# A Mamba-2 and gated-DeltaNet trunk step on one core: one table for Ln and Exp, the query scale folded into the outputs' scale, and the first scan chunk loaded in the projection

## What is computed

```python
q = l2norm(q) * (GDN_DK ** -0.5);  k = l2norm(k)          # rsqrt(sum of squares + EPS)
# for each chunk of tokens and each head, with state S:
o = (q * exp(gcum)) @ S + (q @ k.T * decay) @ v_new
S = S * exp(last) + (k * exp(last - gcum)).T @ v_new
# afterwards
y_gdn = rmsnorm(o, gdn_norm_w) * silu(gate)               # rsqrt(mean of squares + EPS)
```

## Time and profile before

| | us |
|---|---|
| three runs | 3535.12, 3541.09, 3542.61 |
| median | 3541.09 |
| profiled execution | 3537.88 |
| its span, first to last instruction | 3536.1 |
| mixnorm and gates | 0 to 98 |
| projection | 101 to 1151 |
| scan | 1153 to 1973 |
| running sequences | 1977 to 2206 |
| merge, output projection | 2209 to 2635 |
| ffnnorm, up, down, lastnorm | 2636 to 3536 |

### The profile page before, as it was taken

How to read it: one execution, slowest core, us unless ns; L and a number is a source line. 1 busy time by engine, 2 the same in 40 slices (tenths; PEclk the granted TensorE clock), 3 DMA queues, 4 the chain that set the end, 5 groups by cost and what they waited for, 6 DMA issues and landing times. The chain is left out here.

```text
span 3536.1 us, 53776 instructions
## 1 busy us (share of the span) xinstructions
PE 3148.2 (89%) x20442; PEld 2962.7 (84%) x20442; DVE 1559.5 (44%) x2031; ACT 993.9 (28%) x1607; POOL 447.4 (13%) x525
## 2 busy tenths in 40 slices
PE   3799999999999698989999488899886999997996
PEld 2799999999999577777778227899876999997996
DVE  5455555401010467777676443455324322333444
ACT  3232323211211244434334201333213211122333
POOL 1000000000000233333333122000000000000000
PEclk7899999999999799999999666899998999998998
DMA  1222222222222422223320522754401112215432
GB/s 70 78 97 85 97 85 97 97 85 97 85 97 75 101 59 60 59 60 85 86 66 16 165 95 77 256 202 154 150 12 63 59 68 72 72 60 198 168 128 94
DMA packets 223765, 338.78 MB, mean 96 GB/s; under 512 B 146296, under 2 KB 159336, under 8 KB 223248
## 3 DMA queue, kind: packets, MB, share of 16 engines
q1 hardware_dynamic: 217344, 311.73, 27.2%
q0 software_dynamic: 6288, 25.25, 2.0%
HBM read 243.72 MB, written 93.22 MB: 95 GB/s over the span
## 5 line engine op out<-in xcount | busy, mean ns | idle before, releaser
L521 PE MATMUL pps<-h_hi,pwh 128*128 128x358 f32 (+1 forms) x2112 | 687.9, 326 | 13.8 <-DVE pwl L586 13.8
L521 PE MATMUL pps<-h_lo,pwh 128*128 128x358 f32 (+1 forms) x2112 | 689.5, 326 | 0.0
L521 PE MATMUL pps<-h_hi,pwl 128*128 128x358 f32 (+1 forms) x2112 | 686.9, 325 | 0.0
L521 PEld LDWEIGHTS pps<-h_hi,pwh 128*128 128x128 f32 x2112 | 397.0, 188 | 13.9 <-issue 13.9
L521 PEld LDWEIGHTS pps<-h_hi,pwl 128*128 128x128 f32 x2112 | 398.5, 189 | 0.0
L521 PEld LDWEIGHTS pps<-h_lo,pwh 128*128 128x128 f32 x2112 | 397.4, 188 | 0.0
L1585 PE MATMUL u_ps<-f_hi,up_wh 128*128 128x358 f32 (+1 forms) x1056 | 344.6, 326 | 21.3 <-DVE up_wl L1577 21.3
L1585 PE MATMUL u_ps<-f_lo,up_wh 128*128 128x358 f32 (+1 forms) x1056 | 345.2, 327 | 0.0
L1585 PE MATMUL u_ps<-f_hi,up_wl 128*128 128x358 f32 (+1 forms) x1056 | 344.0, 326 | 0.0
L586 DVE TENSOR_TENSOR pwl<-pw,pwh 128x1024 fp32r<-128x1024 f32 x88 | 107.8, 1225 | 506.2 <-ACT pwh L534 500.1
L1585 PEld LDWEIGHTS u_ps<-f_hi,up_wh 128*128 128x128 f32 x1056 | 199.0, 188 | 22.3 <-issue 22.3
(11 more groups left out here) (398 smaller groups left out, 5378.7 us busy)
## 6 DMA issues: line engine op xcount, KB each, us to landing
projected<-pO SPq DMA_DIRECT2D x88, 536.0 KB, 2.8
pw<-in_w_in SPq DMA_DIRECT2D x88, 512.0 KB, 3.4
scan_chunk<-projected SPq DMA_DIRECT2D x10, 3744.0 KB, 16.8
merge_w<-in_w_out SPq DMA_DIRECT2D x72, 512.0 KB, 3.3
down_w<-in_w_down SPq DMA_DIRECT2D x48, 704.0 KB, 4.1
up_w<-in_w_up SPq DMA_DIRECT2D x44, 512.0 KB, 4.4
mixed<-scan_chunk SPq DMA_DIRECT2D x10, 1248.0 KB, 6.5
ffn<-uf SPq DMA_DIRECT2D x22, 536.0 KB, 3.0
```

The lines of the kernel that those rows point to most:

```text
L521: ins = pe.matmul(ps[:, 3 * u + n, 0:cn], l[u][:, k, :], r[:, k, c0:c0 + cn], start=(k == 0 and a == 0), stop=(k == KD - 1 and a == 2))
```

## The change

Four things are done. (1) Each norm, the gates and both scan phases begin on ACT with a load of the table `natural_log_exp_and_others`, which has Ln and Exp (and Copy, Square, Abs). In the scans it stands in place of an Ln of one element, L1111. (2) `o` isn't scaled by the query's scale any more. ACT squares the unscaled `o` as soon as it is complete. DVE squares `rs` of q at the chunk's end (one operation of 104x8), multiplies the mean square by it in `mean_square` (one more operation of 104x8), and forms the product of `rs`, 128 ** -0.5 and `ors` in `normalise` (one more), by which `o` is scaled. `be` grows from two to five rows. (3) SP loads chunk 0 and its three rows of `sel` in the projection, ahead of the "sigmoid" stage, after it has waited for the stores of both buffers; it waits for the load's end at the end of the phase. The buffer lies at the right end of SBUF. (4) The scan counts that load as done and issues only that of chunk 1.

```diff
@@ -178,6 +178,7 @@
             prime(act, squared, ln_done, rstd_done, hi_done)
+            act.preload_act_table_set("natural_log_exp_and_others")
@@ -427,7 +429,7 @@
-def project_phase(nc, d, hi, lo, scratch):
+def project_phase(nc, d, hi, lo, scratch, sums, first, sel):
@@ -454,6 +456,7 @@
         plain = pair("plain", 3)
+        first_in = Loads(nc, "p_first_in", 1, 2)
         zero = Event(nc, "p_zero")
@@ -495,7 +498,17 @@
-            stages(sp, body)
+            def load_first(kind):
+                if kind == "sigmoid":
+                    for u in range(2):
+                        sp.wait_ge(stored.sems[u], stored.at(NSCAN // 2 - 1))
+                    sp.dma_start(sel[3 * H:3 * H + 3, :, :], sums[:, 0:C].rearrange("(a h) n -> a h n", a=3)).then_inc(
+                        first_in.sems[0], 16)
+                    sp.dma_start(first[:, :, :], scratch[0:NSCAN, :, 0:C].rearrange("m p n -> p m n")).then_inc(
+                        first_in.sems[0], 16)
+
+            stages(sp, body, load_first)
+            sp.wait_ge(first_in.sems[0], first_in.at(0))
             for u in range(2):
@@ -623,7 +636,7 @@
-def scan_phase(nc, d, tab, con, scratch, mixed, sums, running):
+def scan_phase(nc, d, tab, con, scratch, mixed, sums, running, chunk0=None):
@@ -649,14 +662,14 @@
         sel = [con["selT"]] + ([] if running else [buf("sel", [P, H, C], BF16)])
-        cd = [buf(f"chunk{u}", [P, NSCAN, c]) for u in range(1 if running else 2)]
+        cd = [buf("chunk0", [P, NSCAN, c])] if running else [chunk0, buf("chunk1", [P, NSCAN, c])]
         kraw, sqr, vb, kn, kbn, kw = (buf(n, [P, HG, P]) for n in ("kraw", "sqr", "vb", "kn", "kbn", "kw"))
...
         mat = buf("mat", [P, 2, HG, c])
-        ss, rs, lg, be = buf("ss", [P, 3, HG]), buf("rs", [P, 2, 2, HG]), buf("lg", [P, 3, HG]), buf("os", [P, 2, HG])
+        ss, rs, lg, be = buf("ss", [P, 3, HG]), buf("rs", [P, 2, 2, HG]), buf("lg", [P, 3, HG]), buf("os", [P, 5, HG])
         ors = buf("ors", [P, HG])
@@ -738,7 +751,7 @@
             E("v_h1", 4 * nseq), E("v_yz", 4), E("v_yms"), E("v_ys", 4))
-        v_rq = E("v_rq")
+        v_rq, v_oqs = E("v_rq"), E("v_oqs")
         v_cm, v_km, v_qm = E("v_cm"), E("v_km"), E("v_qm")
@@ -813,8 +826,9 @@
-                for u in range(2):
-                    load(u, u)
+                sp.sem_inc(loaded.sems[0], 16)
+                sp.sem_inc(sums_in.sems[0], 16)
+                load(1, 1)
                 with sp.Fori(0, NC // 2 - 1) as i:
@@ -1108,8 +1122,7 @@
                   a_ors, a_k, a_kT, a_kbT, a_T, a_X, a_vn)
-            act.activation(lg[:, 0, 0:1], con["ones"][:, 0:1], ACT.Ln)
-
+            act.preload_act_table_set("natural_log_exp_and_others")
             act.wait_ge(zeroed.sem, zeroed.at(0))
@@ -1229,7 +1242,7 @@
                     act.activation(yg, yg, ACT.Copy, scale=yss[0:c, 3, g:g + 1]).then_inc(a_yn.sem, 1)
-                act.wait_ge(v_oq.sem, v_oq.at(r))
+                act.wait_ge(v_o2.sem, v_o2.at(r))
                 act.wait_ge(m_VN.sem, m_VN.at(r))
@@ -1244,7 +1257,7 @@
                   v_kss, v_kn, v_kbn, v_AT, v_qk, v_TT, v_km, v_T, v_TTn, v_yms, v_res, v_o1, v_S0, v_o2,
-                  v_S1, v_rq, v_oq, v_oss, v_oms, v_on, v_ys, v_yg)
+                  v_S1, v_rq, v_oqs, v_oq, v_oss, v_oms, v_on, v_ys, v_yg)
             dve.memset(ss[:, :, :], 1.0)
@@ -1279,12 +1292,19 @@
                 dve.wait_ge(v_oss.sem, v_oss.at(r))
-                dve.tensor_scalar(ss[0:c, 2, :], be[0:c, 1, :], 1.0 / P, EPS, ALU.mult, ALU.add).then_inc(v_oms.sem, 1)
-
-            def normalise(r):
+                dve.wait_ge(v_rq.sem, v_rq.at(r))
+                dve.scalar_tensor_tensor(out=be[0:c, 3, :], in0=be[0:c, 1, :], scalar=1.0 / P ** 2, in1=be[0:c, 2, :],
+                                         op0=ALU.mult, op1=ALU.mult).then_inc(v_oqs.sem, 1)
+                dve.wait_ge(v_oqs.sem, v_oqs.at(r))
+                dve.tensor_scalar(ss[0:c, 2, :], be[0:c, 3, :], EPS, None, ALU.add).then_inc(v_oms.sem, 1)
+
+            def normalise(r, u):
+                dve.wait_ge(a_ors.sem, a_ors.at(r))
+                dve.scalar_tensor_tensor(out=be[0:c, 4, :], in0=rs[0:c, u, 1, :], scalar=float(P) ** -0.5, in1=ors[0:c, :],
+                                         op0=ALU.mult, op1=ALU.mult).then_inc(v_oq.sem, 1)
                 dve.wait_ge(v_oq.sem, v_oq.at(r))
-                dve.wait_ge(a_ors.sem, a_ors.at(r))
-                dve.tensor_tensor(on[0:c, :, :], o[0:c, :, :], bcast(ors[0:c, :], P), ALU.mult).then_inc(v_on.sem, 1)
+                dve.wait_ge(v_o2.sem, v_o2.at(r))
+                dve.tensor_tensor(on[0:c, :, :], o[0:c, :, :], bcast(be[0:c, 4, :], P), ALU.mult).then_inc(v_on.sem, 1)
@@ -1386,7 +1406,7 @@
                 if not first:
-                    normalise(r - 1)
+                    normalise(r - 1, 1 - u)
                 for hb in range(2):
@@ -1469,10 +1489,7 @@
-                dve.tensor_scalar(rs[0:c, u, 1, :], rs[0:c, u, 1, :], float(P) ** -0.5, None, ALU.mult).then_inc(v_rq.sem, 1)
-                dve.wait_ge(v_rq.sem, v_rq.at(r))
-                dve.wait_ge(v_o2.sem, v_o2.at(r))
-                dve.tensor_tensor(o[0:c, :, :], o[0:c, :, :], bcast(rs[0:c, u, 1, :], P), ALU.mult).then_inc(v_oq.sem, 1)
+                dve.tensor_tensor(be[0:c, 2, :], rs[0:c, u, 1, :], rs[0:c, u, 1, :], ALU.mult).then_inc(v_rq.sem, 1)
@@ -1482,7 +1499,7 @@
             mean_square(last_round)
-            normalise(last_round)
+            normalise(last_round, last_place)
             gate_out(last_round, last_place)
@@ -2040,6 +2057,7 @@
                    "naccT": sb("t_naccT", [P, T], BF16)}
+            scanned = to_scan.enter_context(ExitStack())
             with ExitStack() as to_project:
@@ -2052,8 +2070,10 @@
                         "p (b q) -> p b q", b=NB)))
-                project_phase(nc, d, hi, lo, scratch)
-            scan_phase(nc, d, tab, con, scratch, mixed, sums, False)
+                chunk0 = scanned.enter_context(nc.sbuf_tensor("chunk0", [P, NSCAN, C], F32, side="right"))
+                project_phase(nc, d, hi, lo, scratch, sums, chunk0, con["selT"])
+            scan_phase(nc, d, tab, con, scratch, mixed, sums, False, chunk0)
+            scanned.close()
             scan_phase(nc, d, tab, con, scratch, mixed, sums, True)
```

## The result

| | before | changed |
|---|---|---|
| median, us | 3541.38 (3535.12 to 3542.61, 4 runs) | 3518.11 (3516.34 to 3522.13, 4 runs) |
| ratio, 95% interval | | 0.9939 (0.9922 to 0.9957) |
| profiled execution, us | 3537.88, span 3536.1 | 3517.55, span 3515.4 |

The changed kernel is 23 us faster (20.7 by the spans of the two profiled executions). The forecast was 3510 with a range of 3499 to 3522: right in sign and range, 8 us too good by the median, 10 by the sum (30.8 forecast, 20.7 between the two profiled executions).

A forecast was written before the change was run, and what follows sets the result against it. PE (busy 89%) was taken to bound the kernel, the scan being a latency chain partly paced by DVE. Gains of 34.8 us less 4.0 lost gave 30.8, from a median of 3541.1 to 3510 us, range 3499 to 3522.

The forecast's parts named there:

- Loads in the middle chunks: Scan's middle chunks: four table loads of 1.28 us each vanish, but nothing on the path waits for them; gain nothing.
- The scaling of o that goes: Scan's chunk ends: DVE gains 1.2 us at six boundaries inside the code, 7.2; 0 at the three jumps back.
- The small operation in `normalise`: Nine scan chunks: the new product counts in full, 0.2 us each, a cost of 1.9; 5.1 by the nearest row.
- the fourth rival: Scan gives nothing: both small operations wait for GpSimd, another wait replaces L1479's; 3522 us, chance 0.09.
- signs of being wrong: DVE waiting for `ors`, PE waiting at several weight loads, a small operation over 0.3 us, or new low-clock places in the scan.
- The small operation in `mean_square`: Nine scan chunks: the new operation fits into L1282's delay beside GpSimd, cost 0; up to 5.1 if the delay starts anew.
- The clock in the chunks: Scan: low-clock stretches come and go with idle time and can move the sum some 3 us either way; not summed.
- The early chunk: Scan's start: ScalarE waits only for the memset of `h`, gain 13.3 us, plus 1.0 for the Exp load, together 14.3.
- Tile 74: Projection: weights queue behind the early chunk, PE stalls 2.5 us plus 1.5 of low clock; cost 4.0, between 0 and 7.
- A switch costs more than its row: Rival: eight removed table loads on a path each hide another 1.4 us; 3499 us, chance 0.05.
- Norms, gates, tails: Fewer table loads and shorter tails: norms 8.7 us, gates 1.3, scan's tail and running phase 5.2.
- all small terms as worked out: Main case: every term comes as estimated, 3502 to 3517 us, chance 0.68.

The follow-up runs named there:

- e_tables_only: The kernel before with the one table alone, no early chunk, o scaled as before: 3522.36 us, ratio 0.9949 to the kernel before.
- e_reduce: The changed kernel plus an unused `tensor_reduce` behind the small product in `normalise`: 3518.85 us, ratio 0.9947 to the kernel before.
- e_start: The changed kernel with tile 74's weights issued ahead of the early chunk and ScalarE's wait for the memsets removed: 3518.67 us, ratio 0.9945 to the kernel before.
- e_no_fold: The changed kernel with VectorE's scaling of o by the query scale restored and the new small products removed: 3515.17 us, ratio 0.9942 to the kernel before.
- e_no_small: The changed kernel with the query scale's fold rewritten to need no extra small operations in `mean_square` and `normalise`: 3503.53 us, ratio 0.9911 to the kernel before.
- e_best2: The changed kernel with the edits of e_no_small and e_start, and scaling of o by `ors` moved to ScalarE: 3482.38 us, ratio 0.9841 to the kernel before.
- e_fold_only: The kernel before with the folded query scale and its small operations alone: 3546.15 us against 3535.68, ratio 1.0033.
- e_twice: The changed kernel with the small product of `normalise` done twice, the second into an unused row: 3516.42 us, ratio 0.9948 to the kernel before.

## Why the prediction was right, and where it wasn't

- **Loads in the middle chunks: nothing.** Right (e_tables_only).
- **The scaling of o that goes.** Right: 6.3 of 7.2 at the six boundaries, nothing at the jumps back.
- **The small operation in `normalise`: the step that failed.** It read "0.17 us like the small ones plus 0.04 ... I take 0.2, because the stretch of L1287 has no operation that DVE has been seen to wait out". The earlier trace rows showed the opposite: L1287 itself took 1.34 where the last chunk's takes 1.23, and over all ten the median was 1.63. It waited for masks, as its own view in the trace of before says (min/median/max), and so did what was put there. The size was 9.7 for 1.9, above my upper bound of 5.1, since that came from the 0.57 of L1282, which meets the rest of an operation, where L1303 meets the whole of one and sends L1307 into a second. The Trainium skill ("SBUF — State Buffer", section "Who interferes with whom") says that a VectorE instruction with two SBUF inputs contends with a GpSimd instruction that reads SBUF, that who comes first keeps the port for its whole length, and that `tensor_reduce` doesn't contend. The traces and e_reduce agree: L1303 ends 22 to 25 ns behind the end of a mask in nine places, the `tensor_reduce` takes 0.16 us inside one. By that rule the waits of L1303 and L1307 were both to be expected, and the masks' 0.97 priced the first. I hadn't weighed it. It is half the mechanism of the fourth rival (both small operations wait for GpSimd, 3522, chance 0.09; its other half, a new wait in place of L1479's, didn't come), and one of the prediction's own signs of being wrong, a small operation of over 0.3 us.

```profile
L1287 DVE TENSOR_TENSOR scan_sqr<-scan_o,scan_ors x10: 1226/1632/1645, 1269.7 to 1962.0; 104x1024 f32<-104x1024 f32 x10
```

- **The small operation in `mean_square`: 0.** Right in effect, wrong in reason. It didn't fit into the delay of L1282, the delay began anew: the product (L1296) takes 0.57 and L1299 behind it 0.97 (views below; in the last chunk 0.17 each). It cost nothing since VectorE's next steps take PSUM inputs (0.57 us each), don't wait for GpSimd and catch up before the masks begin.

```profile
L1296 DVE SCALAR_TENSOR_TENSOR scan_os<-scan_os x10: 166/570/574, 1243.7 to 1949.3; 104x8 f32<-104x8 f32 x10
L1299 DVE TENSOR_SCALAR scan_ss<-scan_os x10: 171/971/974, 1244.3 to 1949.5; 104x8 f32<-104x8 f32 x10
```

- **The clock in the chunks** was left out of the sum, with "some 3 us either way". It took 8.5; more low clock was another of the signs of being wrong. Not all of it is the fold's: over the same 5294 matmuls of the nine chunks PE is busy 617.7 us in the trace of before, 619.3 to 621.5 in the other three kernels without the fold, whose waits there are the same to 0.6 us, and 623.5 to 628.9 in the six with the fold and its small products. So the fold's share is some 5 to 7 us (4.9 between e_no_fold and the changed kernel, 7 between the means of the two groups), and the rest is a trace of before with less low clock than its like; why, stays open. A step that lengthens a wait of PE in a chunk was priced by the wait alone, though I had charged 1.5 us of clock to the one stall at tile 74, where none came.
- **The early chunk.** At the start 13.4 of 13.3: ScalarE starts right behind the memset of `h`. The 1.0 for the Exp load didn't show: VectorE's wait at L1288 fell from 1.81 to 0.53, but PE's waits in the rest of the chunk are the same; the 2.1 that came are clock.
- **Tile 74.** The mechanism was right and confirmed by moving the weights ahead (e_start). Mis-sized: the chunk landed 15.8 us after its issue (972.7 and 956.9), sooner than the 16.5 to 17.9 of the loads before; the weights landed 1.2 us behind it (973.9), near the 1.4 of the prediction, and PE started 2.5 us later. So 1.2 of stall and not 2.5, and no low clock behind it (1.00), not 1.5.
- **A switch costs more than its row.** No: the load at the scan's tail moved the work behind it by 1.28 (e_tables_only), and the norms, priced by the row too, came at 8.6 for 8.7. By the Trainium skill ("ScalarE: Activation LUTs", "What ACT_TABLE_LOAD costs") a switch would have been 2.66. The trace disagrees: 1.28 in all, and 0.2 us of idle time before eleven loads together.
- **Norms, gates, tails**: 16.5 for 15.2.

The errors partly offset each other: 17 us too much in the chunks, 7 too little elsewhere. That the time still fell in the range is luck to that extent: without the 7 it would have been some 3525 (an estimate, 3518 and 7), outside. The case that the forecast stood on, all small terms as worked out and 3502 to 3517, did not come.

## What to carry to other kernels

Before an operation is added between others, look at what the neighbouring *engine* has in its queue there: a median above the minimum in a line's own view says that the line waits inside its duration, where no idle column shows it. Price a small operation by that, and then follow the delay to the step that gives it back. Better than a cheaper operation is one that isn't needed (e_no_small), or one on an engine that has nothing to do (e_best2).

And add up PE's busy time at equal work: if it grew, the clock took part of the gain. Use more than one trace: here single traces of kernels with the same waits differed by 4 us in it (617.7 to 621.5).

## What the runs showed of the hardware that I hadn't expected

- A VectorE operation of 104x8 values takes 0.16 to 0.17 us alone, 0.57 to 0.97 beside GpSimd's `tensor_tensor`; with two SBUF inputs it ends 20 to 30 ns behind the mask. A `tensor_scalar` with one SBUF input (L1299, 0.97) waits too, a `tensor_reduce` doesn't (0.16).
- The granted clock gave or took as much as the waits did: 11.0 of 13.1 us in e_fold_only, 12.5 of 22.4 in e_no_small, 21.0 of 36.1 in e_best2. Each time the low stretches got longer where PE's waits ahead of them did (6.8 and 3.4 us in most chunks). That they follow from these waits is shown by taking them away (e_no_fold, e_no_small, and the two kernels without the fold). It isn't one to one: e_twice, with PE's wait 0.93 longer, has no longer low stretches, and e_tables_only loses 3.7 us of busy time at the same waits. In the changed kernel PE is busy 14.3 of the 18.5 us before the fall at 1492, and no single wait in them is above 1.81; what exactly PE must do to keep the clock was not tried.
- 1.28 us for a table load is its whole price (PE's wait at the tail, 5.83 for 7.11, in e_tables_only).
